# Two layers written out in place of the loop over layers, with the last norm of layer 0 and the pre-norm of layer 1 interleaved on VectorE

## What is computed

```python
for l in range(DEPTH):                       # DEPTH = 2
    h = rmsnorm(x, mix_norm_pre[l])
    ... = split_columns(h @ w_in[l])         # columns of four mixers
    branches = (y_nsa, y_swa, y_mla, y_fox)  # compressed/selected/window, sliding window, latent, forgetting attention
    merged = sum(sigmoid(h @ w_gate[l, i]) * (y @ w_branch[l, i]) for i, y in enumerate(branches))
    x = x + rmsnorm(merged @ w_out[l], mix_norm_post[l])
    hx = rmsnorm(x, xa_norm_pre[l])
    y = memory_cross_attention(hx, rmsnorm(mem, xa_mem_norm[l]), xa_w_q[l], xa_w_kv[l], xa_w_o[l])
    x = x + rmsnorm(y, xa_norm_post[l])
    hf = rmsnorm(x, ffn_norm_pre[l])
    gu = hf @ ffn_w_in[l]
    y = (silu(gu[..., :D_FF]) * gu[..., D_FF:]) @ ffn_w_out[l]
    x = x + rmsnorm(y, ffn_norm_post[l])
```

## Time and profile before

| what | us |
|---|---|
| median of 3 runs | 2817.48 |
| lowest, highest run | 2807.31, 2840.18 |
| span of the profiled execution | 2851.4 |

### The profile page before, as it was taken

One profiled execution on the slowest core, in us unless ns is written; L12 is line 12 of the kernel. 1 busy time (PEld: TensorE's weight loads), 2 busy tenths in 40 slices (PEclk: granted clock), 3 DMA queues, 4 the chain that ended last, 5 costly groups with the idle time before them and its releaser, 6 DMA issues.

```text
span 2851.4 us, 43271 instructions
## 1 busy us (share of the span) xinstructions
PE 2610.8 (92%) x13794; PEld 2142.9 (75%) x13794; DVE 1574.1 (55%) x3564; ACT 1165.3 (41%) x2432; POOL 126.8 (4%) x183
## 2 busy tenths in 40 slices
PE   1899899999999989999978998898999998999998
PEld 1776777778787878888867677786887886788886
DVE  3247886667375555553234478675755746455522
ACT  1225655464354442222222356463634545322222
POOL 3100000000001010000010000000000010100000
PEclk8779999999999889999987589998999998999999
DMA  4411112212313203333332110122132141133332
GB/s 78 113 42 46 31 39 67 56 56 67 81 53 119 67 23 91 95 101 89 94 92 57 30 38 28 49 67 59 46 82 74 59 126 38 48 95 100 94 94 70
DMA packets 343968, 196.39 MB, mean 69 GB/s; under 512 B 29340, under 2 KB 338704, under 8 KB 343152
## 3 DMA queue, kind: packets, MB, share of 16 engines
q1 hardware_dynamic: 340512, 178.02, 21.9%
q0 software_dynamic: 3280, 16.13, 2.5%
HBM read 186.78 MB, written 7.34 MB: 68 GB/s over the span
## 4 chain that ended last, share of the span: by engine, by line
PE 78%; DVE 9%; issue 5%; ACT 3%; DMA 2%; POOL 1%; DVEq 0%; ACTq 0%; POOLq 0%; SPq 0%
PE acc L1042 59%; PE o_acc L1042 4%; PE turn L1204 3%; PE scores L1042 2%; PE acc L1332 2%; PE scores L1095 2%; DVE ring L1614 1%; DMA w_f<-in_w_in_dram 1%; PE scores L1189 1%; ACT w_hi L727 1%; DVE q_tile L1593 1%; DVE p_lo L1554 1%; DVE w_lo L1457 1%; PE scores L1190 1%; PE o_acc L1117 1%
## 5 line engine op out<-in xcount | busy, mean ns | idle before, releaser
L1042 PE MATMUL acc<-h_hi,w_hi 128*128 128x512 f32 x1888 | 778.9, 413 | 38.9 <-DVE w_lo L1457 22.1
L1042 PE MATMUL acc<-h_lo,w_hi 128*128 128x512 f32 x1888 | 761.5, 403 | 0.0
L1042 PE MATMUL acc<-h_hi,w_lo 128*128 128x512 f32 x1888 | 761.3, 403 | 0.0
L1457 DVE TENSOR_TENSOR w_lo<-w_f,w_hi 128x1024 fp32r<-128x1024 f32 x336 | 411.4, 1224 | 572.5 <-ACT w_hi L727 570.6
L727 ACT ACTIVATE w_hi<-w_f 128x1024 fp32r<-128x1024 f32 x336 | 353.2, 1052 | 323.3 <-PE acc L1042 265.2
L1042 PEld LDWEIGHTS acc<-h_hi,w_hi 128*128 128x128 f32 x1888 | 369.9, 196 | 107.7 <-issue 21.7
L1042 PEld LDWEIGHTS acc<-h_hi,w_lo 128*128 128x128 f32 x1888 | 368.8, 195 | 78.9
L1042 PEld LDWEIGHTS acc<-h_lo,w_hi 128*128 128x128 f32 x1888 | 369.6, 196 | 64.7
L779 ACT ACTIVATE p_hi<-turn 128x256 fp32r<-128x256 f32 (+4 forms) x416 | 163.8, 394 | 339.1 <-PE turn L1204 338.2
L1554 DVE TENSOR_TENSOR p_lo<-turn,p_hi 128x256 fp32r<-128x256 f32 (+4 forms) x416 | 180.5, 434 | 103.8 <-ACT p_hi L779 101.8
L842 ACT ACTIVATE ring<-ring,neg_max 128x256 f32<-128x256 f32 (+4 forms) x416 | 208.5, 501 | 68.3 <-DVE neg_max L1614 67.2
(11 more groups left out here) (260 smaller groups left out, 3743.3 us busy)
## 6 DMA issues: line engine op xcount, KB each, us to landing
w_f<-in_ffn_w_in_dram SPq DMA_DIRECT2D x88, 512.0 KB, 3.8
w_f<-in_w_gate_dram SPq DMA_DIRECT2D x64, 512.0 KB, 3.8
w_f<-in_w_in_dram SPq DMA_DIRECT2D x62, 512.0 KB, 3.9
w_f<-in_w_branch_dram SPq DMA_DIRECT2D x32, 512.0 KB, 3.5
w_f<-in_ffn_w_out_dram SPq DMA_DIRECT2D x32, 512.0 KB, 3.8
w_f<-in_w_out_dram SPq DMA_DIRECT2D x16, 512.0 KB, 3.9
w_f<-in_ffn_w_out_dram SPq DMA_DIRECT2D x16, 384.0 KB, 3.3
x_spill<-trunk POOLq DMA_DIRECT2D x2, 2048.0 KB, 8.4
```

What stands on the lines that cost most here:

```text
L1042: ins = nc.tensor.matmul(dst, a, b, start=(n == 0 and not added), stop=(n == count - 1))
L1457: nc.vector.tensor_tensor(w_lo[:, u % 2, :], w_f32[:, u % 2, :], w_hi[:, u % 2, :].bitcast(F32), ALU.subtract).then_inc(w_ready, 1)
```

## The change

The five loops over layers become Python loops, so that each engine's program holds both layers one behind the other, and the layer is a constant in every wait and address. `wait_apart` becomes one wait for a constant or, within an inner loop, a register expression. VectorE's last norm of layer 0 takes `pre="mix_pre"` with layer 1 as the layer of the rests and splits: misc is split at chunk 1, nsa 0 at chunk 3, and layer 1 starts with row_stats. In `add_to_trunk` the splits of `between` now stand ahead of the rest of the same step, which also holds for the add behind mix_post in both layers (its units are the same as before, given by number).

```diff
@@ wait_apart
-            due = eng.to_reg(value)
-            eng.wait_ge(s_const, 7)
-            eng.wait_ge(signal, due)
+            eng.wait_ge(signal, value)
@@ the programs of sync, gpsimd, scalar and tensor, each
-            with pe.Fori(0, L) as l:
+            for l in range(L):
@@ vector
-            def add_to_trunk(l, name, phase, pre=None, between=()):
+            def add_to_trunk(l, name, phase, pre=None, between=(), pre_layer=None):
 
                 wait_chunk_read(dve, l, phase, KT - 1)
+                of = l if pre_layer is None else pre_layer
                 for c in range(KT + 1 if pre is None else KT + 2):
                     if c < KT:
                         scaled_chunk(l, name, c)
                     if 0 < c <= KT:
                         added_chunk(l, name, c - 1)
-                    if pre is not None and c > 1:
-                        gained_rest(l, pre, c - 2)
                     for at, unit in between:
                         if at == c:
-                            next_unit(l, *unit, 0)
+                            split_rest(of, unit, 0)
+                    if pre is not None and c > 1:
+                        gained_rest(of, pre, c - 2)
...
-            with dve.Fori(0, L) as l:
-                split_rest(l, 0, 0)
-                for c in range(KT):
-                    gained_rest(l, "mix_pre", c)
-                    if c == 1:
-                        next_unit(l, "misc", 0, 0)
+            for l in range(L):
+                if l == 0:
+                    split_rest(l, 0, 0)
+                    for c in range(KT):
+                        gained_rest(l, "mix_pre", c)
+                        if c == 1:
+                            next_unit(l, "misc", 0, 0)
                 row_stats(l, "mix_pre", D)
...
-                add_to_trunk(l, "mix_post", "wout", "xa_pre", ((1, ("xkv", 2)), (2, ("xkv", 3)), (3, ("xq", 0))))
+                add_to_trunk(l, "mix_post", "wout", "xa_pre", ((1, UB["xkv"] + 3), (2, UB["xq"]), (3, UB["xq"] + 1)))
...
-                add_to_trunk(l, "ffn_post", "ffout")
+                if l + 1 < L:
+                    add_to_trunk(l, "ffn_post", "ffout", "mix_pre", ((1, 0), (3, 1)), l + 1)
+                else:
+                    add_to_trunk(l, "ffn_post", "ffout")
```

More of the change, by code:

```diff
@@ L532, in _ @@
             sp.wait_ge(s_slot, 1)
-            with sp.Fori(0, L) as l:
+            for l in range(L):
                 u = UB["misc"]
@@ L690, in power @@
                 pool.tensor_tensor(rstd[:, :], mean_sq[:, :], half_neg[:, :], ALU.pow).then_inc(rstd_ready, 1)
-            with pool.Fori(0, L) as l:
+            for l in range(L):
                 power(l, "mix_pre")
@@ L909, in _ @@
             nc.scalar.activation(cos_sin[r, :], ang[r, 1, :], ACT.Sin).then_inc(s_table, 1)
-            with act.Fori(0, L) as l:
+            for l in range(L):
                 act.wait_ge(misc_raw, l * 64 + 64)
```

## The result

| | before | after |
|---|---|---|
| median | 2832.22 us (20 runs) | 2822.86 us (20 runs) |
| lowest to highest | 2807.31 to 2878.23 | 2790.78 to 2847.84 |
| ratio after / before | | 0.9938, 95% interval 0.9909 to 0.9968 |
| profiled span, mean granted clock | 2851.4 us, 0.931 | 2845.9 us, 0.927 |

The kernel is 0.6% faster, within the 1% that was called no change; the forecast was 13.5 us less (0.48%), and 2822.9 lies in the range of 2782 to 2832. The means of the twenty differ by 15.1 us (95%: within 13.4). The median of before rose from 2817 to 2832 us as runs were added. That alone carries most of the 19 us between the forecast of 2804 and the result.

A forecast was written before the change was run, and what follows sets the result against it. TensorE, busy 2610.8 of 2851.4 us, was taken as the bound. Boundary climb 9.2 plus register arithmetic 4 made 13 us, set against the median 2817.48: 2804 us, range 2782 to 2832.

The forecast's parts named there:

- The boundary climb: Norm and weight stretch between layers: interleaving shortens it from 41.9 to 32.7 us, 9.2 us less.
- The sign named for SP: At the layer boundary, SP's load of nsa 1 goes out about 10 us earlier against the last norm.
- What is late next: In the boundary climb, TensorE and its clock set the end, needing 2.3 us per chunk.
- The clock in the climb: TensorE's low clock at the boundary bounds the climb's gain between -1 and 16 us; 9.2 taken.
- The rule of the Trainium skill: Idle TensorE falls to its lower clock; by this alone, removing the boundary idle would gain 16 us.
- Weights, and the stretch behind: The 102.1 us behind the boundary climb and its w_lo waits stay: nothing, between -2 and 2 us.
- The loops and registers: Written-out loops: VectorE's 1.89 us return counted in the climb; register arithmetic 4 us, ends -3.5 and 26.6.
- rival (2): Register operations in passes that hop between engines are worth 18 us, giving 2790 us; chance 0.12.
- Splits ahead of rests: In the add behind mix_post, both layers: the new order gains nothing, at most 1.1 us lost per layer.
- Rival (1): Low clock eats the boundary gain: 0 to 3 us left with the register term, 2815 us; chance 0.12.
- Rival (3): One more CMP pass falls to the low clock in the typical run, costing 30.0 us: 2834 us; chance 0.10.
- The absolute time: Whole kernel: forecast 2804 us, 13 us below before's then median of 2817.48 us.

The follow-up runs named there:

- e2: Before with only VectorE's loop over layers written out and the last norm interleaved at the boundary; ratio to before 0.9972, median 2833.3 us.
- e3: After with each chunk's rest ahead of the weight split of the same step, as in before; ratio to before 0.9883, median 2817.5 us.
- e4: After plus a filler matmul behind every second block matmul, 30 per layer; ratio to before 1.001, median 2839.5 us.
- e8: After with a sixth gate0 unit as CMP filler, moved from SEL; ratio to before 0.9843, median 2793.3 us.
- e11: The kernel of e8 run again, unchanged; median 2794.8 us.
- e1: After without the interleaving: all loops over layers written out, norms one behind the other; ratio to before 0.9962, median 2830.6 us.
- e5: Before with VectorE's loop over layers alone written out, old order kept; ratio to before 0.9969, median 2837.7 us.
- e6: Before with TensorE's loop over layers alone written out; ratio to before 0.9985, median 2832.4 us.
- e9: Before with the sixth gate0 unit moved from SEL into CMP as in e8, nothing of the change; ratio to before 0.9947, median 2820.5 us.
- e10: e8 with VectorE's split of misc moved behind rstd_lo, ahead of the first scaled chunk; median 2791.2 us.
- e7: After with VectorE's splits of misc and nsa 0 moved into idle stretches of row_stats; ratio to before 0.987, median 2837.2 us.

## Why the prediction was right, point by point

**The boundary climb, 9.2 us (with VectorE's return of 1.89 in it).** Right in place and size. The profile of after alone says 12.7 us (41.9 to 29.2), the value that layer 1's climb would have given. But the climb's length moves with the clock from profile to profile. With the interleaving and the splits at their places it is 29.1, 33.8, 33.5, 31.0, 29.2 and 33.2 us (after, e2, e3, e4, e8, e11), mean 31.6. With the old order it is 41.9, 41.1, 36.8, 43.8 and 41.9 (before, e1, e5, e6, e9), mean 41.1. That is 9.5 us. Part of it is clock: these climbs have 15.4 us of low time in the mean and the others 24.6, which at 0.371 is 3.4 us. At equal low time the interleaving alone is 4.6 to 6.7 us, forecast as 9.2 - 1.9 = 7.3. So that 13.2 us at equal low time match a sum of 13, which counted the climbs at the clocks they met, is in part luck; where the low time is steady the change gives 26.5 us. The sign named for SP came true: its load of nsa 1 goes out 3.3 us behind the first scaled chunk, in before 14.9. What is late next is TensorE, as said: the climb is 27.4 of 29.2 us busy.

**The clock in the climb.** The idle of 11 us is gone, and the mean clock of the climb is 0.82 for 0.71, so 10.5 us of low time for 24.3. It didn't go to zero, and in e2 and e3, with the idle gone too, it is 20.5 us. The rule of the Trainium skill that was weighed (TensorE: Matmul & The Clock Gate, on the clock gate) would have had it all back; the trace agrees with its direction and not with that size, as the feed-forward climbs had suggested.

**Weights, and the stretch behind, nothing.** Nearly right. The stretch is 99.3 us for 102.1, and its waits for the weights' rest are 5.0 us for the 8.7 of the earlier trace rows, outside the 2 us that I allowed; but in layer 0, where no weight was moved, they are 5.9 for 7.4 and the stretch 102.2 for 103.9. The interleaving is not the reason: e1, without it, has 100.8 us and 5.9 in layer 1. Over the profiles but e4's, layer 1's stretch takes 99.1 to 101.9 us with all loops written out and 102.1 to 103.9 with some of them left, so some 2 us of it seem to go with the loops; layer 0's takes 101.7 to 103.5 and 102.1 to 103.9.

**The loops and registers.** Right in sum: 1.9 for the return and 4 for the rest makes 5.9, and e1 measured 6.5 (1.5). TensorE's part was small (1.4), and its branch under cover. The 4 stood on no row, as the nearest one said nothing. The reason that I gave for it, short passes where a dry queue pays, found no support: SEL to FOX, from first to last bias score, took 63.9, 62.2, 83.1, 78.8 and 83.3 us in layer 0 of before and 64.3, 62.6, 84.2, 78.4 and 83.8 in after, though the register operations of L1185 are gone. In after that line (now L1183) has waits and no arithmetic:

```profile
L1183 PEldq EVENT_SEMAPHORE  x104: 51/51/51, 193.1 to 2404.4; - x104
```

So rival (2) falls: the 18 us that it counted for register operations in front of busy engines aren't there, and a wait as it stands takes 51 ns of the queue. Part of the other loops' 3.0 us (e1 less e5) lies in the climbs of xa_pre. ScalarE, ahead of its first chunk there, in before and in after:

```profile
953.50 1.06 ACT L727 ACTIVATE w_hi<-w_f 128x1024 fp32r<-128x1024 f32 x1 [1.44 <-DMA w_f<-in_xa_w_q_dram]
967.66 1.05 ACT L725 ACTIVATE w_hi<-w_f 128x1024 fp32r<-128x1024 f32 x1
```

The wait of 1.44 us for a weight unit is gone. TensorE starts on this climb's products 8.3 and 8.0 us behind the first scaled chunk in before (layer 0 and 1), 8.1 and 7.7 in e5, and 6.9 to 7.0 in every profile with all loops written out: 1.9 us less in both layers together than e5. Which loop brings the unit earlier isn't shown. Where the 1.6 us beyond VectorE's return in e5 lie is not located; it is the size of its error.

**Splits ahead of rests, nothing.** Right (e3). In the climb of xa_pre of layer 0 TensorE starts on the products 6.96 us behind the first scaled chunk in after and in e3 alike.

**Rival (1), the low clock eats it:** no, see above. **Rival (3), one more CMP pass at low clock:** it is what the profiled run of after met (19.5 us in layer 0), and the same kernel meets it in some runs and not in others. Over all runs the two kernels have the same mean clock within its error, so no cost to the change shows. What the long passes cost every version, e8 and e9 show: 11 to 30 us. I had put the cause at the pass's entry. That was half of it: the moment at which the clock comes back sorts the passes (last section), and e8 and e9 show that one more unit in the pass ends the long ones.

**The absolute time** was 19 us off, because the three runs of before stood for its median. Their spread of 33 us, at clocks between 0.93 and 0.95 as now seen, was the warning.

## What to carry to other kernels

Where a norm is followed by the next one, alternate them chunk by chunk on the engine that makes both, and look first at what the consumer waits for in the list of waits: an 11 us wait became 0.65 for a change of order, worth 4.6 to 6.7 us at equal low time, and about half as much again came from straight code on the engine that fed it. When runs of one kernel spread by more than the effect, record the granted clock with each and compare at equal clock; a level was then known to 1.5 us in 2830 with twelve runs. But look at the low time too, since a change can win some, as here, and remove the source of the spread first if you can. And where a pass's length jumps at equal work, try moving real work into it before adding dummy work ahead of it: the first gave 29 us on after and 11 to 24 on before, the second cost 17.

## What the runs showed that was not expected

**CMP has three lengths.** With five filler units, the 18 CMP passes of nine profiles took about 51 us (7 times), 70 (6) or 81 (5), at mean clocks of 1.00 (once 0.97), 0.65 and 0.52. With six, the 8 passes of e8 to e11 took 54.3 to 55.9 us at 0.97 to 1.00. One unit, 24 matmuls of the 265, is the difference between them.

**The moment at which the clock comes back sorts the passes.** In each of the 26 the clock is low over the block matmuls and returns 2.9 to 4.1 us ahead of the pass's first bias score. With five units:

| clock back, us ahead of the first bias score | next fall | pass |
|---|---|---|
| 2.89 to 3.28 (6 passes) | 20.6 to 21.0 us into it, low to its end | 70 us |
| 3.36 to 3.70 (6) | none in it | 51 us |
| 3.74 to 4.01 (5) | 2.8 to 3.1 us into it, low to its end | 81 us |
| 4.14 (1) | 2.7 us into it, for 3.4 us | 52 us |

With six, 2.92 to 3.70 us ahead (5 passes) no fall follows in the pass, and at 3.79 to 4.10 (3) there is one of 3.4 us. The fall near 3 us in, in before's layer 1 (back 4.01 us ahead, at 1572.05) and in e10's layer 0 (3.79 ahead, at 197.40):

```profile
1572.00:1578.80 6.80, 5.42 (x28) 4.48 (x27) 2.69 (x5) 0.90 (x3) 0.00 (x0) 1.00 0.01 2
1578.80:1656.90 78.10, 78.09 (x259) 51.14 (x258) 37.00 (x164) 24.70 (x100) 0.00 (x0) 0.50 0.12 34
204.20:207.60 3.40, 3.40 (x12) 2.30 (x10) 1.64 (x11) 0.99 (x5) 0.00 (x0) 0.50 0.47 141
207.60:257.10 49.50, 49.39 (x278) 33.95 (x276) 34.16 (x151) 25.66 (x97) 0.00 (x0) 1.00 0.16 45
```

In the first the clock stays low though TensorE counts as busy for 78.09 of 78.10 us. So which length comes goes with the moment of the entry, by shifts of under 1 us, and what the pass holds decides whether a fall lasts: at 3.79 us ahead it is over in 3.4 us in e10, at 3.80 ahead it lasts to the end in after's layer 1. No run set the moment on purpose; this is an order found in 26 passes.

**Low time costs 0.37 us per us**, less than the half that an always busy TensorE would pay. The CMP pass alone shows the like: 80.8 us for 50.8 is 30.0 us for some 78 of low time, 0.39 each. TensorE's busy time there goes from 47.1 to 79.4 us and not to twice, and its idle time from 3.7 to 1.4 us: it fills waits.

**POOL's power of 128 x 4 elements doubles beside a VectorE split**, from 1.02 to 1.99 us (once, in e7), though the two share no data; the other 15 powers of e7, with no work of VectorE beside them, take 1.01 to 1.05. An idle stretch of VectorE is not free while POOL works in the critical chain.
